# Expert weights in units of 512 rows x 512 columns, with matmuls 512 columns wide, in a two-layer diffusion backbone

## The reference: what is computed

```
def _swiglu(h, w_gu, w_down):
    gu = h @ w_gu                       # (1024, 2 * 3584)
    f = w_gu.shape[-1] // 2
    return (jax.nn.silu(gu[..., :f]) * gu[..., f:]) @ w_down   # (3584, 1024)

for e in range(N_EXPERTS):              # 8
    out = out + combine[:, e:e + 1] * _swiglu(t, w_gu[e], w_down[e])
```

## Time and profile before

| | us |
|---|---|
| median of 3 runs (2291.38 to 2291.72) | 2291.42 |
| the profiled execution, first to last instruction (its span; the page gives no other time of it) | 2298.1 |
| expert stage within it, first to last expert matmul (1212.3 to 2277.9) | 1065.6 |
| busy in the span: PE, PEld, DVE, ACT, POOL | 2092.4, 1867.6, 1574.7, 1335.5, 94.6 |

### The profile page before, as it was taken

One profiled execution on the slowest core, in us unless ns is written; L12 is line 12 of the kernel. 1 busy time (PEld: TensorE's weight loads), 2 busy tenths in 40 slices (PEclk: granted clock), 3 DMA queues, 4 the chain that ended last, 5 costly groups with the idle time before them and its releaser, 6 DMA issues. The chain is left out here.

```text
span 2298.1 us, 38243 instructions
## 1 busy us (share of the span) xinstructions
PE 2092.4 (91%) x14499; PEld 1867.6 (81%) x14500; DVE 1574.7 (69%) x1994; ACT 1335.5 (58%) x1864; POOL 94.6 (4%) x81
## 2 busy tenths in 40 slices
PE   4999979999997788987869999999999999999997
PEld 2955779998996677766758999898898989989996
DVE  2154345546445666777747898898888889888996
ACT  4145364446445344435447777677676777767775
POOL 0000000000000022223100000000000000000000
PEclk7999989999998899998979999999999999999999
DMA  8359724554542221120347999999899989989994
GB/s 298 111 201 361 244 74 165 179 179 157 183 165 78 75 74 56 56 74 19 103 137 267 337 338 332 326 335 335 306 336 301 358 296 337 337 298 334 342 360 154
DMA packets 387283, 518.02 MB, mean 225 GB/s; under 512 B 10459, under 2 KB 327211, under 8 KB 387115
## 3 DMA queue, kind: packets, MB, share of 16 engines
q1 hardware_dynamic: 387115, 515.57, 66.3%
HBM read 514.49 MB, written 1.05 MB: 224 GB/s over the span
## 5 line engine op out<-in xcount | busy, mean ns | idle before, releaser
L1715 DVE TENSOR_TENSOR lo<-raw,hi 128x1024 fp32r<-128x1024 f32 x880 | 1073.2, 1231 | 435.5 <-ACT hi L1243 283.8
L668 PE MATMUL bank<-hi,xh_t 128*128 128x256 f32 x2912 | 839.0, 288 | 51.1 <-issue 21.1
L1263 ACT ACTIVATE hi<-raw 128x1024 fp32r<-128x1024 f32 x672 | 710.7, 1062 | 261.0 <-PE bank L670 258.6
L670 PE MATMUL bank<-hi,xl_t 128*128 128x256 f32 x2912 | 833.7, 286 | 0.0
L669 PE MATMUL bank<-lo,xh_t 128*128 128x256 f32 x2912 | 833.6, 286 | 0.0
L668 PEld LDWEIGHTS bank<-hi,xh_t 128*128 128x128 f32 x2912 | 567.9, 195 | 62.4 <-issue 47.8
L669 PEld LDWEIGHTS bank<-lo,xh_t 128*128 128x128 f32 x2912 | 568.0, 195 | 6.0 <-issue 1.9
L670 PEld LDWEIGHTS bank<-hi,xl_t 128*128 128x128 f32 x2912 | 567.5, 195 | 0.0
L1243 ACT ACTIVATE hi<-raw 128x1024 fp32r<-128x1024 f32 x208 | 218.5, 1063 | 300.0 <-PE bank L670 281.9
L668 PE MATMUL bank<-hi,hth 128*128 128x512 f32 x624 | 258.0, 413 | 0.0
L670 PE MATMUL bank<-hi,htl 128*128 128x512 f32 x624 | 244.7, 392 | 0.0
(11 more groups left out here) (264 smaller groups left out, 1831.7 us busy)
## 6 DMA issues: line engine op xcount, KB each, us to landing
raw<-in_moe_gu_w_dram SPq DMA_DIRECT2D x224, 1024.0 KB, 6.3
raw<-in_moe_down_w_dram SPq DMA_DIRECT2D x112, 1024.0 KB, 6.1
raw<-in_ada_w_dram SPq DMA_DIRECT2D x24, 2048.0 KB, 8.9
raw<-in_ffn_gu_w_dram SPq DMA_DIRECT2D x44, 1024.0 KB, 5.1
raw<-in_ffn_down_w_dram SPq DMA_DIRECT2D x22, 1024.0 KB, 4.9
raw<-in_ssm_in_w_dram SPq DMA_DIRECT2D x16, 1024.0 KB, 5.3
raw<-in_ssm_out_w_dram SPq DMA_DIRECT2D x8, 1024.0 KB, 6.6
raw<-in_mix_in_w_dram SPq DMA_DIRECT2D x5, 1024.0 KB, 12.7
```

The costliest lines, as they stand in the source:

```text
L668: mm(o, a_hi, w_hi, start=first, stop=False, **kw)
L670: return mm(o, a_lo, w_hi, start=False, stop=last, **kw)
L1263: A_(hi[:, p % SPL, :], raw[:, u, (i % 2) * PIECE:(i % 2 + 1) * PIECE], ACT.Copy).then_inc(hi_ready, 1)
L1715: TT(lo[:, p % SPL, :], raw[:, u, h * PIECE:(h + 1) * PIECE], hi[:, p % SPL, :].bitcast(F32), ALU.subtract).then_inc(lo_ready, 1)
```

## The change

An expert now has 7 steps of 512 hidden columns. A unit is 512 x 512 for gate and up (4 row blocks of 128, two units per step and kind; runs of 2 KB in DRAM); a down unit stays 256 x 1024, two per step. A piece is still 128 x 1024 elements, two row blocks x 512 columns. Gate and up matmuls are 512 columns wide and fill PSUM bank 4 and bank 5; SiLU has one buffer instead of two. Transposes come four at a time. Slots and gather move to steps 3 and 5 of 7. The expert pieces have semaphores of their own (`m_hi`, `m_lo`, `m_used`), and the first four are split between the norms before the router instead of in the output projection. The gathered rows lie in contiguous views of `xh_t` and `xl_t`. Expert 0 is also written out on SP. The dense FFN keeps its code, with the expert's offsets taken out.

```diff

-MOE_STEPS = D_FF_EXPERT // UCOL
-MOE_UNITS = 3 * MOE_STEPS
+MCOL = 512
+MOE_STEPS = D_FF_EXPERT // MCOL
+MOE_UNITS = 6 * MOE_STEPS
...
+def moe_order(n):
+
+    order = []
+    for j in range(n + 2):
+        if j < n:
+            order += [("g", j, 0), ("g", j, 1), ("u", j, 0), ("u", j, 1)]
+        if j >= 2:
+            order += [("d", j - 2, 0), ("d", j - 2, 1)]
     return order
...
-        mpjunk = o0.take(D_MODEL)
         mxn = [o0.take(D_MODEL) for _ in range(2)]
         mt32, mt32b = o0.take(D_MODEL), o0.take(D_MODEL)
+        mpjunk = mt32b
...
-        msg = [o0.take(UCOL) for _ in range(2)]
-        mhb = [o0.take(UCOL) for _ in range(2)]
+        msg = o0.take(MCOL)
+        mhb = [o0.take(MCOL) for _ in range(2)]
+        xgh, xgl = (v3(a[:, 0:KC * P], KC) for a in (xh_t, xl_t))
...
-        J_GATHER = 9
+        J_SLOTS, J_GATHER = 3, 5
...
+                for i, (k, j, h) in enumerate(order_moe):
                     u = U_MOE + i
 
-                    sp.wait_ge(lo_ready, it * MOE_PIECES + 2 * (S_MOE + i - RAW + 1))
+                    if first and i < RAW:
+                        sp.wait_ge(lo_ready, 2 * (S_MOE + i - RAW + 1))
+                    else:
+                        sp.wait_ge(m_lo, it * MOE_PIECES + 2 * (i - RAW + 1))
                     if k == "d":
-                        sp.dma_start(rawv(u, 2), dn[j * UCOL:(j + 1) * UCOL, :].rearrange("(t p) n -> p t n", p=P)
+                        r = j * MCOL + h * (MCOL // 2)
+                        sp.dma_start(rawv(u, 2), dn[r:r + MCOL // 2, :].rearrange("(t p) n -> p t n", p=P)
                                      ).then_inc(raw_landed[slot(u)], 16)
                     else:
-                        sp.dma_start(rawv(u, 8), wcols(gu, j * UCOL + (D_FF_EXPERT if k == "u" else 0), UCOL)
+                        c = j * MCOL + (D_FF_EXPERT if k == "u" else 0)
+                        sp.dma_start(rawv(u, 4), wcols(gu[h * 4 * P:(h + 1) * 4 * P, :], c, MCOL)
                                      ).then_inc(raw_landed[slot(u)], 16)
 
-            with sp.Fori(0, N_EXPERTS) as e:
-                expert_weights(e, e)
+            expert_weights(0, 0, True)
+            with sp.Fori(1, N_EXPERTS) as e:
+                expert_weights(e, e, False)
...
+            def mpiece(p, a):
+
+                return hi[:, p % SPL, a:a + 512], lo[:, p % SPL, a:a + 512]
+
+            def moe_swiglu(it, at_step):
+
+                ud, cd, td = it * MOE_PIECES, C_MOE + it * MOE_STEPS, T_MOE + it * MOE_STEPS
+                for j in range(MOE_STEPS + 2):
+                    for kind in ("g", "u") if j < MOE_STEPS else ():
+                        o = bank[4 if kind == "g" else 5][:, :]
+                        for h in range(2):
+                            p = 2 * pos_moe[(kind, j, h)]
+                            if h == 0:
+                                pe.wait_ge(sil_done if kind == "g" else h_done, cd + j)
+                            for t in range(4):
+                                k = 4 * h + t
+                                if t % 2 == 0:
+                                    pe.wait_ge(m_lo, ud + p + t // 2 + 1)
+                                m = tok3(o, xgh[:, k, :], xgl[:, k, :], *mpiece(p + t // 2, t % 2 * MCOL),
+                                         first=(k == 0), last=(k == KC - 1))
+                                if t % 2:
+                                    m.then_inc(m_used, 1)
+                    if 1 <= j <= MOE_STEPS:
+                        pe.wait_ge(h_done, cd + j)
+                        pe.wait_ge(ht_lo, td + max(j - 2, 0))
+                        for q in range(4):
+                            m = pe.transpose(bank[6 + (j - 1) % 2][:, q * P:(q + 1) * P],
+                                             mhb[(j - 1) % 2][:, q * P:(q + 1) * P], ident)
+                        m.then_inc(ht_t, 1)
+                    at_step(j)
+                    if j >= 2:
+                        pe.wait_ge(ht_lo, td + j - 1)
+                        if j == 2:
+                            pe.wait_ge(y_evac, Y_MOE + 2 * it)
+                        for h in range(2):
+                            p = 2 * pos_moe[("d", j - 2, h)]
+                            for t in range(2):
+                                pe.wait_ge(m_lo, ud + p + t + 1)
+                                a = (2 * h + t) * P
+                                for half in range(2):
+                                    m = tok3(bank[half][:, :], hth[:, j % 2, a:a + P], htl[:, j % 2, a:a + P],
+                                             *mpiece(p + t, half * 512),
+                                             first=(j == 2 and h == 0 and t == 0),
+                                             last=(j == MOE_STEPS + 1 and h == 1 and t == 1))
+                                m.then_inc(m_used, 1)
...
+            def hi_moe(p, it, first=False):
+
+                u = slot(U_MOE + p // 2)
+                if p % 2 == 0:
+                    act.wait_ge(raw_landed[u], landed_moe(p // 2, it))
+                if first and p < SPL:
+                    act.wait_ge(piece_used, P_MOE - SPL + p + 1)
+                else:
+                    act.wait_ge(m_used, it * MOE_PIECES + p - SPL + 1)
+                A_(hi[:, p % SPL, :], raw[:, u, (p % 2) * PIECE:(p % 2 + 1) * PIECE], ACT.Copy).then_inc(m_hi, 1)
...
             norm_a(12)
             norm_a(13)
+            hi_moe(0, 0, True)
+            hi_moe(1, 0, True)
             norm_b(12)
             norm_b(13)
+            hi_moe(2, 0, True)
+            hi_moe(3, 0, True)
...
+                    if j < MOE_STEPS:
+                        look(("g", j, 0))
+                        look(("g", j, 1))
+                        act.wait_ge(m_used, ud + 2 * pos_moe[("g", j, 1)] + 2)
+                        act.wait_ge(h_done, cd + j)
+                        A_(msg, bank[4][:, :], ACT.Silu).then_inc(sil_done, 1)
+                        look(("u", j, 0))
+                        look(("u", j, 1))
+                    if 1 <= j <= MOE_STEPS:
+                        act.wait_ge(ht_t, td + j)
+                        if j >= 3:
+                            act.wait_ge(m_used, ud + 2 * pos_moe[("d", j - 3, 1)] + 2)
+                        A_(hth[:, (j - 1) % 2, :], bank[6 + (j - 1) % 2][:, :], ACT.Copy).then_inc(ht_hi, 1)
...
             norm_a(12)
             norm_a(13)
+            lo_moe(0, 0)
+            lo_moe(1, 0)
             norm_b(12)
             norm_b(13)
+            lo_moe(2, 0)
+            lo_moe(3, 0)
...
+                    if j < MOE_STEPS:
+                        for k in ("g", "u"):
+                            for h in range(2):
+                                look((k, j, h))
+                        dve.wait_ge(sil_done, cd + j + 1)
+                        dve.wait_ge(m_used, ud + 2 * pos_moe[("u", j, 1)] + 2)
+                        dve.wait_ge(ht_t, td + max(j - 1, 0))
+                        TT(mhb[j % 2], msg, bank[5][:, :], ALU.mult).then_inc(h_done, 1)
+                    if 1 <= j <= MOE_STEPS:
+                        dve.wait_ge(ht_hi, td + j)
+                        TT(htl[:, (j - 1) % 2, :], bank[6 + (j - 1) % 2][:, :], hth[:, (j - 1) % 2, :].bitcast(F32),
+                           ALU.subtract).then_inc(ht_lo, 1)
...
-                    if j == MOE_STEPS // 2 and after:
+                    if j == J_SLOTS and after:
                         slots(e + 1, it + 1, posm)
                     if j == MOE_STEPS and after:
 
-                        dve.wait_ge(piece_used, P_MOE + it * MOE_PIECES + 2 * pos_moe[("u", MOE_STEPS - 1)] + 2)
+                        dve.wait_ge(m_used, ud + 2 * pos_moe[("u", MOE_STEPS - 1, 1)] + 2)
                         gather_split(it + 1)
-
-                swiglu(S_MOE, it, 1, MOE_STEPS, pos_moe, C_MOE, T_MOE, msg, mhb, look, at_step)
-                dve.wait_ge(piece_used, P_MOE + (it + 1) * MOE_PIECES)
+                    if j >= 2:
+                        look(("d", j - 2, 0))
+                        look(("d", j - 2, 1))
+                dve.wait_ge(m_used, (it + 1) * MOE_PIECES)
                 dve.tensor_copy(yexp[:, 512:1024], bank[1][:, :]).then_inc(y_evac, 1)
```

More of the change, by code:

```diff
@@ L1223, in _ @@
                         it = e + N_EXPERTS
-                        for s, before, per in ((piece_used, P_MOE + it * MOE_PIECES, MOE_PIECES),
+                        for s, before, per in ((m_used, it * MOE_PIECES, MOE_PIECES),
                                                (ht_t, T_MOE + it * MOE_STEPS, MOE_STEPS),
@@ L1662, in gather_mod, with expert, look @@
                 i.then_inc(gat_mod, 1)
-            def expert(it, after):
-                def look(i):
-                    if i + SPL < MOE_PIECES or after:
-                        hi_moe(i + SPL, it)
-                def at_step(j):
+            def expert(it, first, after):
+                def look(key):
+                    for p in range(2 * pos_moe[key] + SPL, 2 * pos_moe[key] + SPL + 2):
```

(38 more changed lines are left out.)

91 lines of the change are left out of this document (32 added, 59 removed).

## The result

| us | before | after |
|---|---|---|
| median (lowest to highest) of 4 runs | 2291.57 (2291.38 to 2293.65) | 2222.57 (2220.96 to 2227.09) |
| profiled execution; its span | span 2298.1 | 2220.96; 2219.2 |
| first to last expert matmul | 1065.6 | 997.1 |

A forecast was written before the change was run, and what follows sets the result against it. PE's own instruction stream was taken to set the time. The terms -34.7 - 2.8 - 1.0 + 4.9 + 0.7 gave -32.9 us, taken off the median 2291.42: 2258.5 us, range 2246 to 2280.

The forecast's parts named there:

- item 7: PE's loop over experts: the five stops of some 4.6 us and their half clock stay, cost 0.
- item 1: Gate/up matmuls: 336 of 512 columns replace 672 of 256, gaining 4.47 us per expert, 34.7 us in all.
- loop stops improve too: Case of an even larger gain than forecast if DMA, clock and PE's loop stops also improve; chance 0.02.
- Rival (a): Matmul cost: only columns count, with gate/up spacing above 0.235 us as its sign; chance 0.06.
- six half-clock stretches: Some 3.4 us each, at the start and behind PE's five stops, where wider gate/up matmuls gain nothing; 3% of this work.
- Items 2 to 5: Transposes gain 2.8 us; ACT and DVE work stays covered; bunched DVE work costs PE time; single buffers cost 0.
- item 4: Bunched DVE work: in the last gate/up step's wake PE waits 0.7 us, in seven experts, +4.9 us; elsewhere little or nothing.
- rival (c): DVE's split chain takes over in each step, slower than before: 2298 to about 2338 us; chance 0.08.
- Item 6: Weight DMA: transfers with 2 KB gate/up rows stay covered by PE's time; cost 0, bounds 0 and 2 us per expert.
- Rival (b): DMA takes over if 2 KB rows are no quicker, losing up to 2 us per expert: 2275 us; chance 0.12.
- Item 8: Step into the experts: the last expert split leaves the output projection's end, gaining 1.0 us.

The follow-up runs named there:

- b_unroll: The kernel before with PE's loop over experts 1 to 6 written out, nothing else changed: 2264.45 us, ratio 0.9873.
- a256_unroll: The changed kernel with each 512-wide gate/up matmul made as two of 256 and PE's loop written out (part of the products not kept): 2262.83 us, ratio 0.9864.
- a_row1k: The changed kernel with each gate/up unit loaded by two transfers of 256 columns, so DRAM rows are 1 KB again: 2227.34 us, ratio 0.9693.
- a_split_later: The changed kernel with DVE splitting the first piece of the last down group ahead of the gathered rows instead of behind them: 2226.86 us, ratio 0.9698.
- a_unroll: The changed kernel with PE's loop over experts written out: 2228.17 us, ratio 0.9711.
- a_pair: The changed kernel with two experts per trip of PE's loop, so two jumps back instead of five: 2234.03 us, ratio 0.9728.
- before_again: The kernel before, unedited, run once more for a second profile: one run of 2289.57 us.
- b_hint_late: The kernel before with a hint announcing PE's jump back placed ahead of the last two down groups: 2286.53 us, ratio 0.9963.
- a256_loop: The changed kernel with each 512-wide gate/up matmul made as two of 256, PE's loop kept (part of the products not kept): 2284.66 us, ratio 0.9955.

## Why the prediction was right in direction and wrong in size

**The failed step is item 7.** It said "PE stays inside the same six-trip loop: five stops of some 4.6 us with their half clock. Cost 0, bounds 1 us less or more each". The loop stayed and the stops vanished. I had read the stops as a property of a jump and had bounded them at 1 us each; they were a property of a jump in a trip of 1969 PE records, and the change cuts that to 1263. In the changed kernel the branch takes 0.2 us instead of 6.5. I counted the matmuls that go (item 1) and did not ask what their disappearance does to the length of the code. A shorter loop body was absent from the rivals too, apart from 0.02 for "loop stops improve too".

The gain by its parts, from the same two traces: the jumps cost 32.2 us before and 0 after. Without jumps a period is 129.88 (b_unroll) and 125.22, so 4.66 less, for eight experts some 37 (the last one gives 4.2). Together some 69, where the stages differ by 68.5 and the medians by 69. The forecast 32.9 belongs to the part of some 37; the other half of the gain was not forecast at all.

1. *Item 1, width.* 4.45 per expert measured alone against 4.47. The spacing of 0.227 us holds when all gate/up matmuls go to one bank (twelve intervals from 1453.83 to 1456.55 in the changed kernel). The rows' fixed cost of 13.3 ns per matmul was right: 4.45 us over 336 matmuls are 13.2. Rival (a) falls: if only columns counted, 672 matmuls of 256 columns would take as long as 336 of 512. No run shows that; they took 4.45 us more. The window of the earlier trace rows does not bear out 18 matmuls in 3.4 us, since it counts those that overlap its ends; the starts in it are 0.213 us apart, which is 2 x (0.120 - 0.0133) at a granted clock of 0.50, so the reading holds. The six half-clock stretches that I set aside became one, at the start (granted clock 0.97 in 1200 to 1300, 1.00 in the later windows), which gives back about 1 us.
2. *Items 2 to 5.* Between b_unroll (129.88) and a256_unroll (129.67) lies all of the change but the width, both without a jump: 0.21 us better per expert. The prediction has 0.35 gained on transposes and 0.7 + 0.1 lost behind DVE, so 0.45 worse. The mis-sized term is the 0.7 of item 4: the wait is there, once per expert and where it was put, but it is 0.49 - 0.23 = 0.26 us (0.36 without the loop). That is 3 us of the miss. DVE's chain fitted everywhere else, so rival (c) falls.
3. *Item 6.* Cost 0, as said. I expected gate/up windows above 360 GB/s; an expert's 44 MB in 125.2 us are 352, and the trace has 352 over the stretch, and with 1 KB rows (a_row1k) the period is the same, so demand by PE sets that number, not row length. (At 2.86 and 2.71 us per unit item 6's sum for an expert is 118 us, not 119; nothing hangs on it.) With 1 KB rows the share of the DMA engines rises from 95.8% to 103.5%, and the time stays. Rival (b) falls.
4. *Item 8.* From the projection's last matmul to the transposes of the norm: 11.26 us before, 10.32 after, so 0.94 for 1.0.

## What to carry to other kernels

A stop at each loop jump with the label "issue" or with an accidental releaser is worth two looks: at the duration of the branch's record on the loop's line, and at the instruction queues in the DMA view. Where the branch took microseconds and packets ran through the whole loop (1969 records a trip, 6.5 us; 2523, 4.5 us), a shorter trip (fewer, wider instructions: 1263 records, 0.2 us; a split loop was not tried) or writing the loop out took away the stop and, where there was one, the half clock behind it. When a change removes instructions from a loop, ask what the shorter body does at its jump before carrying the old stops over as a constant. Price the edit with the loop written out as well as with it: only so do the two effects separate.

## What the runs showed that I had not expected

- A trip of 1263 or 1557 PE records runs with no instruction packet on q8 from its second pass on and no stop at the jump (the one packet of a_split_later and a_row1k in 1440 to 2080 comes at 1444 and 1446, at the end of the first pass); one of 1935, 1969 or 2523 has packets throughout and stops of 2.5 to 5.7 us between two starts. Straight code has 24 packets in 640 us at 125.3 us an expert (4.7 x 16 KB = 77 KB) and 36 at 129.9 (7.3 x 16 KB = 120 KB); over the 6018 and 9185 PE records of those 640 us (a_unroll, b_unroll) that is some 64 bytes a record. By that the trips without packets reach up to some 100 KB (1557 records) and those with packets begin by 124 KB (1935), an estimate from these runs.
- Instruction packets that land in straight code cost at most 0.1 us per expert (a_unroll, 125.3 against 125.2); PE stopped for them only at jumps.
- The clock follows the stops unevenly. Behind the 5.66 us stop the granted clock is 0.50 for 3.9 us, behind both stops of a_pair (2.97 and 3.10) it stays 1.00, and so it does behind the 3.94 us one of before_again; behind one of 2.50 us in b_hint_late it falls to 0.50, and of the 3.1 us stops in a256_loop one has a half clock behind it and one has not.
- Left open: why the packet that ends a stop starts 1.9 us behind the branch once and 4.75 another time, why 1.4 to 1.6 us pass between its landing and the next record, and why a hint at the head of the trip does nothing while one close to the branch does a little. No version here beat the changed kernel.
